# A decoder step with 32 experts on one core: two weight matrices kept as 8 KB runs, and first products that read their columns from two places

## What is computed

```python
def _hier_moe(x, rg_w, rg_b, re_w, re_b, w1, w3, w2):
    ...                       # gate[t, group, expert]: two entries of a token are not zero
    for gi in range(N_GROUPS):
        h = jax.nn.silu(einsum('td,edf->tef', x, w1[e0:e1])) * einsum('td,edf->tef', x, w3[e0:e1])
        h = h * gate[:, gi, :, None]
        y = y + einsum('tef,efd->td', h, w2[e0:e1])
    return y
```

## Time and profile before

| | |
|---|---|
| median of 3 runs | 1463.87 us |
| lowest and highest | 1459.5 and 1464.09 us |
| span of the profiled execution | 1460.4 us |
| PE busy | 1280.5 us (88%) |
| DVE, ACT, POOL busy | 648.9, 409.1, 469.0 us |
| read from and written to memory | 295.45 and 27.01 MB |
| expert loads | 96 DMAs of 1024 KB, median 12.8 us from issue to landing |
| mean granted clock | 0.938 |

### The profile page before, as it was taken

One profiled execution on the slowest core, in us unless ns is written; L12 is line 12 of the kernel. 1 busy time (PEld: TensorE's weight loads), 2 busy tenths in 40 slices (PEclk: granted clock), 3 DMA queues, 4 the chain that ended last, 5 costly groups with the idle time before them and its releaser, 6 DMA issues. The chain is left out here.

```text
span 1460.4 us, 32259 instructions
## 1 busy us (share of the span) xinstructions
PE 1280.5 (88%) x13766; PEld 984.4 (67%) x13766; DVE 648.9 (44%) x1339; ACT 409.1 (28%) x856; POOL 469.0 (32%) x398
## 2 busy tenths in 40 slices
PE   7988899999999999999999989978636999986960
PEld 6777689889879979978988978767533333332320
DVE  2749763354345246335435535445362322211228
ACT  3143134234325224323423422422100222211214
POOL 1616272372254236327237327323001111111100
PEclk9999899999999999999999999989857999998995
DMA  9887537736834844853783562490088999999978
GB/s 272 251 214 237 165 94 240 233 103 191 274 103 155 270 129 133 258 179 100 242 252 103 175 204 90 137 125 19 21 293 291 356 319 379 371 364 370 372 283 323
DMA packets 275079, 317.28 MB, mean 217 GB/s; under 512 B 15332, under 2 KB 253488, under 8 KB 274536
## 3 DMA queue, kind: packets, MB, share of 16 engines
q1 hardware_dynamic: 262520, 277.51, 60.5%
q10 hardware_dynamic: 5792, 20.78, 4.2%
q0 software_dynamic: 6624, 16.92, 3.0%
HBM read 295.45 MB, written 27.01 MB: 221 GB/s over the span
## 5 line engine op out<-in xcount | busy, mean ns | idle before, releaser
L1533 PE MATMUL psum<-arena 128*128 128x256 f32 (+3 forms) x1536 | 308.3, 355 | 2.6 <-issue 2.6
L1533 PEld LDWEIGHTS psum<-arena 128*128 128x128 f32 x1536 | 255.7, 193 | 32.3 <-issue 3.2
L2378 PE MATMUL psum<-arena 128*64 128x512 f32 (+1 forms) x832 | 169.9, 620 | 21.7 <-DMA arena<-in_exp_w 21.7
L1236 DVE COPY_PREDICATED arena<-arena,psum 128x128 f32<-128x128 int32 x280 | 85.3, 305 | 139.1 <-PE psum L1722 132.2
L1529 PE MATMUL psum<-arena 128*128 128x128 f32 x1152 | 139.5, 281 | 3.4 <-issue 1.9
L1529 PEld LDWEIGHTS psum<-arena 128*128 128x128 f32 x1152 | 135.0, 197 | 6.1 <-issue 5.6
L669 POOL TENSOR_TENSOR arena<-arena 128x768 f32<-128x768 f32 (+1 forms) x32 | 59.1, 1846 | 238.7 <-ACT arena L900 238.7
L2378 PEld LDWEIGHTS psum<-arena 128*64 128x64 f32 (+1 forms) x832 | 53.4, 136 | 121.5 <-issue 119.5
L1491 PE MATMUL psum<-arena 64*64 64x64 f32 x3264 | 116.5, 223 | 4.7 <-issue 2.0
L1491 PEld LDWEIGHTS psum<-arena 64*64 64x64 f32 x3264 | 104.6, 136 | 21.7 <-issue 13.9
L1801 PE MATMUL psum<-arena 128*128 128x256 f32 x512 | 118.4, 391 | 0.8 <-ACT arena L977 0.8
(11 more groups left out here) (399 smaller groups left out, 1953.9 us busy)
## 6 DMA issues: line engine op xcount, KB each, us to landing
arena<-in_w_in SPq DMA_DIRECT2D x96, 1024.0 KB, 6.4
arena<-in_exp_w SPq DMA_DIRECT2D x96, 1024.0 KB, 12.8
arena<-in_w_out SPq DMA_DIRECT2D x32, 1024.0 KB, 5.9
arena<-in_w_in SPq DMA_DIRECT2D x24, 512.0 KB, 5.3
arena<-y_d SPq DMA_DIRECT2D x16, 512.0 KB, 10.9
arena<-in_x_prompt ACTq DMA_DIRECT2D x15, 512.0 KB, 5.9
arena<-in_w_in SPq DMA_DIRECT2D x8, 576.0 KB, 4.9
arena<-in_w_in SPq DMA_DIRECT2D x8, 560.0 KB, 4.4
```

What stands on the lines that cost most here:

```text
L1236: ins = v.copy_predicated(h3(att_b)[:, h:h + 2, :], b3(q_mask[4 * half + j], 2, 64), new)
L1533: ins = mm(b[:, 0:n], hT[:, c, :], w[:, c, 0:n], start=(c == 0), stop=(c == KC - 1))
L2378: ins = mm(bank[2 + q % 2][at:at + width, :], xT[q % 2][:, c, at:at + width], w13[n % NB][:, c, :], start=(c == 0), stop=(c == KC - 1))
```

## The change

`w13[b]` becomes `[p, m, c, n]` with m = 0 for w1 and m = 1 for w3: first all 2048 numbers of w1 of a partition, then all 2048 of w3. In memory the 8 rows of a partition are consecutive, so a load of w1 or w3 is now one run of 8 KB for each partition on both sides, where it was eight runs of 1 KB in the buffer. The first products read `w13[n % NB][:, :, c, :]`: 256 numbers of w1 and 256 of w3 that stand 8 KB further on. Number, order, size and waits of the DMAs and of the matmuls stay the same on every engine, and the PSUM columns too; `flat` is the same memory as before. The loop for overflowing experts reads its stationary side from the new places.

```diff
-    w13 = [wall[:, b * W:b * W + KC * 512].rearrange("p (c n) -> p c n", c=KC) for b in range(NB)]
+    w13 = [wall[:, b * W:b * W + KC * 512].rearrange("p (m c n) -> p m c n", m=2, c=KC) for b in range(NB)]
...
-    flat = [w13[b].rearrange("p c n -> p (c n)") for b in range(NB)]
+    flat = [w13[b].rearrange("p m c n -> p (m c n)") for b in range(NB)]
...
+    def w13_flat(buf, m):
+
+        return w13[buf][:, m].rearrange("p c n -> p (c n)")
+
     def load_w(eng, e, buf):
-        eng.dma_start(w13[buf][:, :, 0:256], A["exp_w1"][0, e].rearrange("(p c) n -> p c n", c=KC)).then_inc(w13_in(buf), 16)
-        eng.dma_start(w13[buf][:, :, 256:512], A["exp_w3"][0, e].rearrange("(p c) n -> p c n", c=KC)).then_inc(w13_in(buf), 16)
+        eng.dma_start(w13_flat(buf, 0), A["exp_w1"][0, e].rearrange("(p c) n -> p (c n)", c=KC)).then_inc(w13_in(buf), 16)
+        eng.dma_start(w13_flat(buf, 1), A["exp_w3"][0, e].rearrange("(p c) n -> p (c n)", c=KC)).then_inc(w13_in(buf), 16)
...
     def load_13(sp, e, buf, sem):
-        w1v = A["exp_w1"][0].rearrange("e (p c) n -> e p c n", c=KC)
-        w3v = A["exp_w3"][0].rearrange("e (p c) n -> e p c n", c=KC)
-        sp.dma_start(w13[buf][:, :, 0:256], w1v[bass.ds(e, 1)]).then_inc(sem, 16)
-        sp.dma_start(w13[buf][:, :, 256:512], w3v[bass.ds(e, 1)]).then_inc(sem, 16)
+        for m, name in enumerate(("exp_w1", "exp_w3")):
+            src = A[name][0].rearrange("e (p c) n -> e p (c n)", c=KC)
+            sp.dma_start(w13_flat(buf, m), src[bass.ds(e, 1)]).then_inc(sem, 16)
...
-                        ins = mm(bank[2 + q % 2][at:at + width, :], xT[q % 2][:, c, at:at + width],
-                                 w13[n % NB][:, c, :], start=(c == 0), stop=(c == KC - 1))
+                        ins = mm(bank[2 + q % 2][at:at + width, :].rearrange("p (m n) -> p m n", m=2),
+                                 xT[q % 2][:, c, at:at + width], w13[n % NB][:, :, c, :], start=(c == 0), stop=(c == KC - 1))
...
-                        ins = mm(bank[2][:, j * P:(j + 1) * P], w13[1][:, c, j * P:(j + 1) * P],
+                        ins = mm(bank[2][:, j * P:(j + 1) * P], w13[1][:, j // 2, c, (j % 2) * P:(j % 2 + 1) * P],
```

## The result

The changed kernel takes 1447.58 us in the median of 4 runs (1446.37 to 1449.86), the kernel before 1462.15 us in 4 runs beside it (1459.5 to 1464.09). The ratio is 0.9902, 95% interval 0.9881 to 0.9922: 14 us, 1.0% faster. The forecast was 1447.4 us. The profiled span is 1445.2 us where it was 1460.4. Three single executions in the last set of runs (e9 to e11 and their before), of 2225.6 to 7151.9 us, are left out of the medians and ratios.

What follows compares the result with a forecast made beforehand. PE was taken to bound the first quads and the DMA queue the last. Of 26.6 us that weights cost PE, 6.6 and 0 to 4.9 remain; 16.5 off 1463.87 gives 1447.4 us, range 1438 to 1459.

Steps and rivals of the forecast that it cites:

- What bounds: Expert stage: PE sets the pace of the first quads, the DMA queue that of the last; weights cost PE 26.6 us.
- Transfers: Loads of w1 and w3: 8 KB runs take 2.52 us instead of 3.00, 0.96 us less for each expert.
- From the queue to PE: Stepping 23 quads with seven buffers: waits fall to 6.6 us at quads 18 and 19; gain 15.1 to 20.0, taken 16.5.
- Waits and clock: PE groups after waits: waits up to 2.84 us left 7.09 us, 4.25 did not; 0 to 4.9 us for the clock.
- First products in two places: First-product matmuls reading 2 x 256 numbers 8 KB apart: no cost taken, at worst 47 ns a record.
- The slower rival: PE pays 47 ns on each first-product record for the second piece: 8 us slower, 1472 us; chance 0.06.
- Rate unchanged: Rival on the weight loads: 1 KB runs are already long enough, time stays 1463.9 us; chance 0.09.
- SP and gathers: SP's shorter issues give nothing; gathers and scatters land 2.1 us later, hidden by 14 us of cover.

Runs made afterwards that it cites:

- e9: The changed kernel itself, run again beside two others on one chip; 1447.97 us, 0.9896 of before.
- e11: The changed kernel with w2 issued behind the next expert's w1 and w3, and w2 as an 8 KB run, second look; 1437.01 us, 0.9828 of before.
- e1: The changed kernel's two-place reads, but w1 and w3 arriving in 1 KB pieces, four DMAs an expert; 1462.56 us, 0.9993 of before.
- e7: The changed kernel with the second half of w2 not loaded from expert 11 on; 1438.17 us, 0.9838 of before.
- e2: The changed kernel with w1 and w3 interleaved in groups of two rows, pieces of 2 KB; 1453.28 us, 0.9929 of before.
- e3: The changed kernel with w1 and w3 interleaved in groups of four rows, pieces of 4 KB; 1450.92 us, 0.9917 of before.
- e5: The changed kernel with SP issuing w2 behind the next expert's w1 and w3; 1437.15 us, 0.9833 of before.
- e6: The kernel before (1 KB pieces) with SP issuing w2 behind the next expert's w1 and w3; 1457.02 us, 0.9965 of before.
- e10: The changed kernel with w2 issued behind the next expert's w1 and w3, run again on one chip; 1438.96 us, 0.9846 of before.
- e4: The changed kernel with w2 also as one 8 KB run, its two transposes reading every other column; 1447.30 us, 0.9895 of before.

## Why the prediction was right

**The number.** The gain was forecast at 16.5 us and came out at 14.6 in medians. That 1447.4 and 1447.58 us agree to 0.2 us is luck: the forecast started from 1463.87 us, the median of three runs, where four give 1462.15, and the 1.7 us by which it started too high nearly cancel the 1.9 us by which the gain fell short. In the runs of after and of e1 to e11 the time is 1.75 to 1.94 us over its own span, and 1460.4 + 1.8 would have been the better start. The mechanism held by itself, in the stage:

**What bounds.** Right. PE in the first quads and the queue in the last: e7 takes only bytes from the queue and gets 9 us more than the change (10.4 us from the first to the last quad), e1 keeps the queue's rate and gets nothing.

**Transfers.** Right, in size too. 2.52 us for a load was read from runs of 4096 and 9200 bytes; with 8 KB the full stretch of 1250 to 1350 us runs at 417 GB/s, w2 and gathers included, which is 2.51 us for 1 MB.

**From the queue to PE.** The step that turned 27 us of transfer into 16.5 us of time held best: two waits left, before quads 18 and 19, of 7.4 us where 6.6 were reckoned, and one group at the lower clock (2.7 us, within 0 to 4.9). From the first quad's start to the last copy of second products on DVE (1413.05 and 1397.81 us, the rows of the chain) the stage lasted 301.2 us before and 284.6 now: 16.6 us, and 26.6 - 7.4 - 2.7 is 16.5. The two waits share out otherwise, 4.83 and 2.60 us and not 3.3 each. The three fitted values (2.5 us from release to first byte, 1.6 us from last byte to PE, 1.1 us for a gather or scatter) were the weak point of that step, for they were set by one kernel's waits and no run measures them singly; e2, e3, e5 and e6 tried them at other rates and in another order, and were met within 2 us each. The span shrank by 15.2 and not 16.5 us, since the first quad started 1.35 us later in this profile (1113.21 against 1111.86). SP's first expert load already came 1.29 us later (1066.98 against 1065.69 us), before anything that the change touches.

**Waits and clock.** The reasoning was too simple. The prediction ordered the waits by length, with no fall of the clock up to 2.84 us and one at 4.25. A wait of 3.08 us left the group at 7.09 us in e2 (the row here), while one of 1.96 us was followed by 8.72 us in e5 (the row there), and one of 1.94 us by 8.76 in e10.

```profile
1315.79 7.09 PE L2381 MATMUL psum<-arena 128*64 128x512 f32 x32 [3.08 <-DMA arena<-in_exp_w]
```
The length of the last wait alone doesn't decide; what does was not tried. That one group and not none or two ran slow was inside the range of 0 to 4.9 us, and the prediction had no way to tell.

**First products in two places.** Right: the least and median of 832 records are the same, and e1 shows it by time. The slower rival rested on the 47 ns between the fastest and the median record of a matmul in six pieces; two pieces of 256 cost nothing in these records. What lengthens the median of the one in six pieces of 64 was not tried.

**Rate unchanged.** Refuted by e2 and e3, where the rate grows with the piece. The Trainium skill's page "DMA: Bandwidth & Descriptors", section Specifications, calls 512 bytes enough for line rate; here pieces of 1 KB reached 349 and of 8 KB 411 to 422 GB/s, so the measurement decides against it. It decides as well against the bound near 358 GB/s that the page's section "Where 436 GB/s comes from" sets for loads from memory, as far as this program goes, which runs on one core; the same section also has a measured 425 GB/s, and 417 lies close to that.

**SP and gathers.** SP's issues got shorter; that this by itself is worth nothing, as reckoned, was not tried alone. Gathers land 2.5 us later (2.1 reckoned) and are covered.

## What to carry to other kernels

Where a DMA queue is the pace, look at the shorter of the two runs of each transfer, in memory and in the buffer: a layout that makes 1 KB pieces into 4 KB ones gives a sixth more bandwidth where they move alone (349 and 411 GB/s), and the matmul that then reads two places pays nothing on its moving side. Reckon what of it arrives by stepping the consumer and the buffers through, not by the bytes, and then read what the issuing queue waits for: after this change most of the rest was an order in which urgent loads stood behind a wait for something later, worth another 7 us. Such a wait costs where the queue has pauses, and that can be far ahead of the place where the consumer waits. And when two kernels differ by a few us in one stage, take the stage's length from the traces beside the medians: the part ahead of it moved by up to 7 us between runs here.

## What was not expected of the hardware

- A stationary operand read with a step of two float32 loads slower, 206 against 141 ns in the median (e4), and it lengthened a quad by 0.08 us, while a moving operand in two pieces 8 KB apart is free (592 and 592 ns). The record's length alone says little: other lines of the same program load 128 columns in 190 ns whose numbers stand in a row (L1533 of after).
- With 1 KB pieces two of an expert's three issues hold SP for 3.5 and 4.0 us in the median (L1985 and L1989 of before), with 8 KB pieces each takes some 0.4 us (L1988 and L1992 of after), and longer pieces let SP run further ahead. At the stage's start the first issue of over 2 us is the 5th with pieces of 1 KB, the 6th with 2 KB, the 8th with 4 KB, the 10th with 8 KB and the 12th with w2 in 8 KB too (before, e2, e3, after, e4), so the queue's room goes neither by DMAs nor by bytes; by what it goes was not tried.
- Whether the clock falls isn't told by the length of the wait before (1.96 us with a fall in e5, 1.94 in e10, 3.08 us without in e2).
